# Sparse attention: adding the causal masks on VectorE in the score bank, and a new order of VectorE's work in a head

## The reference

```python
s_c = q @ k_cmp.T * scale            # 31 compressed keys
p_c = masked_softmax(s_c, cmp_end <= t)
s_s = q @ k_sel.T * scale            # selected branch
p_s = masked_softmax(s_s, key <= t)
s_w = q @ k_win.T * scale            # window branch
p_w = masked_softmax(s_w, key <= t)
o = g0 * (p_c @ v_cmp) + g1 * (p_s @ v_sel) + g2 * (p_w @ v_win)
```

## Time and profile before

| | us |
|---|---|
| median of 3 runs | 977.13 (976.85 to 977.81) |
| the profiled execution | 977.82, its span 976.0 |
| PE busy in the span | 943.1 (97%) |
| DVE, ACT, POOL busy | 474.0, 418.0, 442.7 |
| mean granted clock of PE | 0.990 |

### The profile page before, as it was taken

One profiled execution on the slowest core, in us unless ns is written; L12 is line 12 of the kernel. 1 busy time (PEld: TensorE's weight loads), 2 busy tenths in 40 slices (PEclk: granted clock), 3 DMA queues, 4 the chain that ended last, 5 costly groups with the idle time before them and its releaser, 6 DMA issues. The chain is left out here.

```text
span 976.0 us, 15705 instructions
## 1 busy us (share of the span) xinstructions
PE 943.1 (97%) x5718; PEld 821.5 (84%) x5718; DVE 474.0 (49%) x1523; ACT 418.0 (43%) x973; POOL 442.7 (45%) x589
## 2 busy tenths in 40 slices
PE   6999998999999999999999999999899999999798
PEld 6888888999999997888888878888688888888676
DVE  5231028787777774211201126668546666666411
ACT  5353236777777774322422423444233333333310
POOL 2453427887877853333433336668611111111131
PEclk9999999999999999999999999999989999999899
DMA  6332221110111012122652122322100000000031
GB/s 210 110 119 86 79 79 47 47 48 23 36 47 47 13 44 87 44 87 84 142 134 88 44 87 87 93 87 87 43 1 1 2 1 1 2 1 2 1 118 54
DMA packets 39253, 58.84 MB, mean 60 GB/s; under 512 B 8693, under 2 KB 22282, under 8 KB 39178
## 3 DMA queue, kind: packets, MB, share of 16 engines
q1 hardware_dynamic: 39136, 57.84, 18.9%
q10 hardware_dynamic: 42, 0.01, 0.0%
HBM read 55.62 MB, written 2.10 MB: 59 GB/s over the span
## 5 line engine op out<-in xcount | busy, mean ns | idle before, releaser
L1359 POOL TENSOR_TENSOR w_lo<-w_raw,w_hi 128x2048 fp32r<-128x2048 f32 (+1 forms) x26 | 118.4, 4553 | 158.9 <-ACT w_hi L1133 158.9
L95 PE MATMUL bank<-w_hi,h_hi 128*128 128x512 f32 (+2 forms) x480 | 187.2, 390 | 3.0 <-POOL w_lo L1287 1.9
L97 PE MATMUL bank<-w_hi,h_lo 128*128 128x512 f32 (+2 forms) x480 | 183.3, 382 | 0.0
L96 PE MATMUL bank<-w_lo,h_hi 128*128 128x512 f32 (+2 forms) x480 | 183.3, 382 | 0.0
L95 PEld LDWEIGHTS bank<-w_hi,h_hi 128*128 128x128 f32 x480 | 90.3, 188 | 21.3 <-issue 2.6
L97 PEld LDWEIGHTS bank<-w_hi,h_lo 128*128 128x128 f32 x480 | 90.2, 188 | 17.1
L96 PEld LDWEIGHTS bank<-w_lo,h_hi 128*128 128x128 f32 x480 | 90.3, 188 | 15.6
L1925 POOL TENSOR_TENSOR o_c<-o_c,o_sw 128x256 f32<-128x256 f32 x16 | 11.7, 732 | 171.8 <-DVE o_c L1994 171.8
L1133 ACT ACTIVATE w_hi<-w_raw 128x2048 fp32r<-128x2048 f32 (+1 forms) x26 | 49.2, 1891 | 78.9 <-PE bank L97 78.9
L1841 PE MATMUL bank<-kvr,probT 128*128 128x65 f32 x640 | 80.5, 273 | 0.0
L95 PE MATMUL bank<-w_hi,o_hi 128*128 128x512 f32 x192 | 78.2, 407 | 2.1 <-PEq L2023 2.1
(11 more groups left out here) (277 smaller groups left out, 2193.1 us busy)
## 6 DMA issues: line engine op xcount, KB each, us to landing
w_raw<-in_nsa_w_in SPq DMA_DIRECT2D x10, 1024.0 KB, 5.0
w_raw<-in_mla_w_in SPq DMA_DIRECT2D x8, 1024.0 KB, 5.1
w_raw<-in_mla_w_out SPq DMA_DIRECT2D x8, 1024.0 KB, 5.2
w_raw<-in_nsa_w_in SPq DMA_DIRECT2D x8, 984.0 KB, 5.0
w_raw<-in_mla_w_uq SPq DMA_DIRECT2D x8, 576.0 KB, 4.1
w_raw<-in_mla_w_ukv SPq DMA_DIRECT2D x16, 256.0 KB, 2.7
w_raw<-in_nsa_w_out SPq DMA_DIRECT2D x4, 1024.0 KB, 5.0
w_raw<-in_mla_w_in SPq DMA_DIRECT2D x4, 704.0 KB, 5.6
```

The lines of the kernel that those rows point to most:

```text
L95: nc.tensor.matmul(out, a[0], b[0], start=start, stop=False)
L96: nc.tensor.matmul(out, a[0], b[1], start=False, stop=False)
L97: return nc.tensor.matmul(out, a[1], b[0], start=False, stop=stop)
L1359: nc.gpsimd.tensor_tensor(w_lo[g % 2][:, :, 0:width], w_raw[g % 2][:, :, 0:width], w_hi[g % 2][:, :, 0:width].bitcast(F32), ALU.subtract). ...
```

## The change

The six mask matmuls of a head are gone from PE. The last large term of a unit now ends it (stop=True, s_done). A new f32 tile "after" (0 on and below the diagonal, NEG above it, in the turned layout) is made once by GpSimd, and DVE adds it in place in the score bank to the first 128 columns of each branch, one instruction a unit, with a new semaphore s_masked on which ACT's exponential waits. The second branch of units 4 and 5 now starts its accumulation with start=True. On DVE the order of a head becomes: masks 0 and 1, low(n+1), masks 2, 3 and 4, maximum 0 of n+1, mask 5, maximum 1, compressed_max, maxima 2 and 3, compressed_turned, maxima 4 and 5, compressed_sum, leave of tiles 0 to 2, leave of tile 3, compressed_leave.

```diff
--- before.py
+++ after.py
@@ -1699,6 +1699,8 @@
                 c_s = at_slab("c_s", 31, [P, NT, NC])
                 c_e = at_slab("c_e", 31.5, [P, NT, NC])
                 c_eT = at_slab("c_eT", 58, [P, P])
+                after = at_slab("after", 59.25, [P, P])
+                after_set, s_masked = sem("after_set"), sem("s_masked")
                 rowmax = at_slab("rowmax1", 58.5, [P, 2, NT, 2])
                 scored = [at_slab(f"scored{a}", 60 + 2 * a, [P, SEQ]) for a in range(2)]
                 coef = at_slab("coef1", 58.625, [P, NT, 2])
@@ -1762,7 +1764,7 @@
                         j, keys = block_of[u][0], slice(block_of[u][0] * P, (block_of[u][0] + 1) * P)
                         left = left_of(j)
                         dst = score_bank[(U * n + u) % 3][:, w * left:(w + 1) * left]
-                        nc.tensor.matmul(dst, kT_hi[0:DK, b, g, keys], qT_lo[a][:, j * P:], start=w == 0, stop=False)
+                        nc.tensor.matmul(dst, kT_hi[0:DK, b, g, keys], qT_lo[a][:, j * P:], start=True, stop=False)
                         nc.tensor.matmul(dst, kT_lo[:, b, g, keys], qT_hi[a][0:DK, j * P:], start=False, stop=False)
 
                     def large_term(n, u, w, b):
@@ -1771,15 +1773,8 @@
                         j, keys = block_of[u][0], slice(block_of[u][0] * P, (block_of[u][0] + 1) * P)
                         left, rows = left_of(j), DK + 1 + b
                         dst = score_bank[(U * n + u) % 3][:, w * left:(w + 1) * left]
-                        nc.tensor.matmul(dst, kT_hi[0:rows, b, g, keys], qT_hi[a][0:rows, j * P:], start=False, stop=False)
-
-                    def mask(n, u):
-
-                        j, branches = block_of[u]
-                        nb, left = len(branches), left_of(j)
-                        dst = score_bank[(U * n + u) % 3][:, 0:nb * left].rearrange("p (b c) -> p b c", b=nb)[:, :, 0:P]
-                        nc.tensor.matmul(dst, causal, identb[:, :].unsqueeze(1).to_broadcast([P, nb, P]), start=False,
-                                         stop=True).then_inc(s_done, 1)
+                        return nc.tensor.matmul(dst, kT_hi[0:rows, b, g, keys], qT_hi[a][0:rows, j * P:], start=False,
+                                                stop=True)
 
                     def scores(n, u):
                         k = U * n + u
@@ -1787,7 +1782,8 @@
                             pe.wait_ge(exp_done, k - 2)
                         for w, b in enumerate(block_of[u][1]):
                             small_terms(n, u, w, b)
-                            large_term(n, u, w, b)
+                            last = large_term(n, u, w, b)
+                        last.then_inc(s_done, 1)
 
                     def start_scores(n):
 
@@ -1801,9 +1797,7 @@
                         if n == 0:
                             pe.wait_ge(rows_set, 1)
                         for u in range(2):
-                            large_term(n, u, 0, u)
-                        for u in range(2):
-                            mask(n, u)
+                            large_term(n, u, 0, u).then_inc(s_done, 1)
 
                     def compressed_scores(n):
                         a = n % 2
@@ -1855,16 +1849,12 @@
                             turn_q(n + 1)
                         scores(n, 2)
                         scores(n, 3)
-                        mask(n, 2)
-                        mask(n, 3)
                         values(n, 0)
                         scores(n, 4)
-                        mask(n, 4)
                         if more:
                             first_scores(n + 1, 0)
                             first_scores(n + 1, 1)
                         scores(n, 5)
-                        mask(n, 5)
                         compressed_scores(n)
                         values(n, 1)
                         if more:
@@ -1891,7 +1881,7 @@
                         j, branches = block_of[u]
                         wide = len(branches) * left_of(j)
                         at = at_of[j, branches[0]]
-                        act.wait_ge(s_done, k + 1)
+                        act.wait_ge(s_masked, k + 1)
                         nc.scalar.activation(probT[n % 2][:, at:at + wide], score_bank[k % 3][:, 0:wide],
                                              ACT.Exp).then_inc(exp_done, 1)
 
@@ -1919,6 +1909,10 @@
                     o = Order(pool, pool_s)
                     o.link(nc.gpsimd.memset(kT_hi[DK:DK + 2, :, :, :].bitcast(F32), 1.0))
                     nc.gpsimd.memset(kT_hi[DK:DK + 1, 1, :, :].bitcast(F32), 0.0).then_inc(rows_set, 1)
+                    pool.wait_ge(rows_set, 1)
+                    o.link(nc.gpsimd.memset(after[:, :], 0.0))
+                    nc.gpsimd.affine_select(out=after[:, :], in_=after[:, :], compare_op=ALU.is_ge, fill=NEG, base=0,
+                                            pattern=[[1, P]], channel_multiplier=-1).then_inc(after_set, 1)
                     for n in range(H):
                         pool.wait_ge(o_left, 2 * n + 2)
                         pool.wait_ge(cv_left, n + 1)
@@ -1995,25 +1989,41 @@
                                                 c_coef[:, :].unsqueeze(2).to_broadcast([P, NT, DV]),
                                                 ALU.mult).then_inc(cv_left, 1)
 
+                    def mask(n, u):
+                        j, branches = block_of[u]
+                        nb, left = len(branches), left_of(j)
+                        dve.wait_ge(s_done, U * n + u + 1)
+                        at = score_bank[(U * n + u) % 3][:, 0:nb * left].rearrange("p (b c) -> p b c", b=nb)[:, :, 0:P]
+                        nc.vector.tensor_tensor(at, at, after[:, :].unsqueeze(1).to_broadcast([P, nb, P]),
+                                                ALU.add).then_inc(s_masked, 1)
+
                     low(0)
                     for u in range(U):
                         maximum(0, u)
+                    dve.wait_ge(after_set, 1)
                     for n in range(H):
                         more = n + 1 < H
+                        for u in range(2):
+                            mask(n, u)
                         if more:
                             low(n + 1)
+                        for u in range(2, 5):
+                            mask(n, u)
+                        if more:
                             maximum(n + 1, 0)
+                        mask(n, 5)
+                        if more:
                             maximum(n + 1, 1)
                         compressed_max(n)
                         if more:
                             maximum(n + 1, 2)
                             maximum(n + 1, 3)
-                        compressed_sum(n)
-                        leave(n, slice(0, 3), o_most, 2 * n + 1)
                         compressed_turned(n)
                         if more:
                             maximum(n + 1, 4)
                             maximum(n + 1, 5)
+                        compressed_sum(n)
+                        leave(n, slice(0, 3), o_most, 2 * n + 1)
                         leave(n, slice(3, 4), o_last.unsqueeze(1), 2 * n + 2)
                         compressed_leave(n)
```

## The result

The changed kernel takes 1033.47 us (median of 4 runs, 1027.6 to 1037.62), the kernel before beside it 976.99: a ratio of 1.0576 (95% interval 1.0548 to 1.0604). Slower by 5.8%, where 0.8% faster was forecast. The profiled execution took 1037.62, its span is 1035.7.

The account below looks back on a forecast made before the run. PE was taken to bound the heads' stage: 11.37 us of work plus stalls of 0.42 and 0.44 gave 12.23 a head. Taking 0.48 gained over 15 transitions plus the last head, 7.5 us, gave 969.6 from 977.13; range 964 to 978.5.

Parts of the forecast that it names:

- The walk: Timing of one head's hand-overs between PE, ACT and DVE: 12.23 us a head after the change, from 12.75 in the trace.
- a granted clock that falls in the new gaps: Listed sign that the forecast is wrong: PE's clock dropping in the two new waits, ahead of units 3 and 5.
- T: Zero point of a head: start of ACT's activation that puts the maxima into the query's rows.
- Masks off PE: Removing six identity mask matmuls a head with their loads from PE's path saves 0.57 us a head.
- The gap: PE's wait for DVE's last maximum, ahead of turning the maxima (line 1755), goes with DVE's new order: 0.81 us a head.
- Masks on DVE: Six additions a head in PSUM, 0.29 us at 128x128 and 0.42 at 128x256, raising DVE's load by 2.0 us.
- rival 1: DVE's mask chain costs more than it frees: slower, about 982.5 us at double durations; chance 0.12 beyond 979.1.
- Exponential 0: ACT's first exponential of a head, behind DVE's mask 0: forecast to run from T+1.73 to T+2.33, before from T+1.47.
- the stall ahead of unit 3: New PE wait for the bank of exponential 0, forecast at 0.42 us a head.
- The stall ahead of unit 5: New PE wait for exponential 2, late because low(n+1) stands ahead of mask 2 on DVE; forecast at 0.44 us a head.
- the work: PE's work alone in a head, without new stalls: 12.75 - 0.57 - 0.81 = 11.37 us.
- Rival 3: PE is not held by the exponentials: both stalls vanish, 11.37 us a head, 957 us (half: about 963); chance 0.08.

Follow-up runs that it names:

- e9: Changed kernel plus eight throwaway zero matmuls a head on TensorE, queued in the gap ahead of unit 5; 973.1 us, ratio 0.9958.
- e7: Changed kernel with zero mask matmuls back on TensorE for units 4 and 5 only; 970.83 us, ratio 0.9931.
- e1: Kernel before, masks still on TensorE, with only compressed_sum and the leave of tiles 0 to 2 moved behind maxima 4 and 5; 969.86 us, ratio 0.9926.
- e4: Changed kernel with mask 2 moved ahead of low(n+1) on VectorE; 965.7 us, ratio 0.9885.
- e8: e4 with the previous head's leave of tile 3 and compressed_leave moved behind masks 0 and 1; 962.42 us, ratio 0.9864.
- e2: Changed kernel with VectorE's old order (compressed_sum and leave ahead of compressed_turned and maxima 4 and 5); 1034.57 us, ratio 1.0603.
- e6: Changed kernel with zero mask matmuls back on TensorE for units 0 and 1 only; 1021.83 us, ratio 1.0451.
- e5: Changed kernel with all six zero mask matmuls a head back on TensorE and low(n+1)'s subtraction done twice; 1024.34 us, ratio 1.0477.

## Why the prediction was wrong

**What failed.** The walk gave a period, and the sum turned it into a time at the granted clock of before. I had named "a granted clock that falls in the new gaps" among the things that would prove me wrong, yet gave it neither a chance nor a price. The reasoning that let it pass was that the earlier trace rows read 1.00 although each head had a gap of 0.74 us, so two of 0.4 seemed harmless. But the old gap lay behind the compressed values and ahead of the turning of the maxima and the 512-column matmuls of the next head, and the new one lies just ahead of the smallest matmuls of the head (128, 64, 32 and 65 columns), from which, moreover, the masks' 256-column matmuls of units 4 and 5 had been taken. I read this as: where the gap lies counts, and not its length alone. That is argued and not shown, since no run moved a gap of one length with TensorE's other work unchanged.

**Its price** could have been bounded from the trace of the kernel before, whose stage starts at a granted clock of 0.50 (708 to 714). Matmuls of 512 columns start 0.43 us apart there, and 0.23 at 1.00:

```profile
709.92 0.63 PE L1766 MATMUL bank<-qT_hi,kT_lo 96*128 96x512 f32 x1
710.35 0.63 PE L1765 MATMUL bank<-qT_lo,kT_hi 96*128 96x512 f32 x1
...
789.08 0.39 PE L1766 MATMUL bank<-qT_hi,kT_lo 96*128 96x512 f32 x1
789.31 0.65 PE L1774 MATMUL bank<-qT_hi,kT_hi 97*128 97x512 f32 x2
```

So a head lies between 12.2 us and nearly twice that. Measured: 17.02 us a head here, 12.33 in e9 (760.12 to 772.45 of its T rows), so 4.7 us a head; 14 heads make 65.7 us, and the profiled executions of the two are 1037.6 and 972.6, 65.0 apart. The clock is the whole difference between these two. At full clock the forecast of 969.6 stands beside e9's 973.1 and e7's 970.8.

**Masks off PE, 0.57 us a head.** From e1's 12.28 to e4's 11.87, and e4 still has 0.14 us of waiting ahead of unit 3 in it (the load there comes at 786.19, 0.32 behind the one before at 785.87, where 0.18 is the step; in the starts of the matmuls it costs 0.10). So 0.51 to 0.55: right, or 0.06 too much at most.

**The gap, 0.81 us.** Mis-sized: e1 measures 0.47. Of the 0.34 too much, 0.10 is a slip in the sum: 800.82 less 800.00 less one load step of 0.11 is 0.71. Most of the rest is that I gave the two records of line 1826 a load step of 0.11 each. They are plain f32 with 256 columns. TensorE's matmuls at that place in the kernel before, then in e1, where nothing is waited for, and e1's loads:

```profile
799.72 0.65 PE L1826 MATMUL bank<-v_diag,c_eT 128*128 128x256 f32 x2
800.71 0.60 PE L1755 MATMUL bank<-ident,rowmax 128*2 128x128 f32 x4 [0.34 <-DVE rowmax L1947]
```

```profile
796.97 0.65 PE L1826 MATMUL bank<-v_diag,c_eT 128*128 128x256 f32 x2
797.46 0.60 PE L1755 MATMUL bank<-ident,rowmax 128*2 128x128 f32 x4
```

```profile
796.91 0.30 PEld L1826 LDWEIGHTS bank<-v_diag,c_eT 128*128 128x128 f32 x2
797.24 0.52 PEld L1755 LDWEIGHTS bank<-ident,rowmax 128*2 128x2 f32 x4
```

The columns of line 1755 start 0.49 us behind those of line 1826 in e1, where the sum's own steps put them 0.33 apart, and the four loads of line 1755 need 0.52 for the 0.30 in the earlier trace rows: they queue behind columns that still run. So 0.16 us of what I took for idle was TensorE streaming columns of line 1826. The matmul record itself had the nearer number, an idle of 0.34 us where the record of loads has 0.74. The Trainium skill, page FP8 and Floating Point Precision, section TensorE Precision Notes, says that true FP32 makes four passes through the array. The trace agrees: the matmuls of 512 columns above start 0.23 us apart, so four passes of 256 are an estimated 0.46, for the 0.49 measured. The rule would have corrected that part of the term.

**Masks on DVE.** 292 and 433 ns for 0.29 and 0.42: right, so rival 1 did not arise. The result is on its side of zero, but its mechanism isn't the cause. The higher overhead on PSUM that the prediction cites from the Trainium skill, page Perfetto Trace Analysis, section Optimizing Scalar/DVE Operations, does not show here for an f32 addition that reads and writes PSUM.

**The walk.** Exponential 0 came at T+1.51, not 1.73: T itself is 0.3 us later behind the last maximum (line 1826 again), so VectorE's leftovers were out sooner, and the stall ahead of unit 3 was 0.14 at the load and 0.10 in the matmuls, not 0.42. The stall ahead of unit 5 is 0.43 in the record of loads, but part of that lies under columns still running. Its cost is read from unit 5's third matmul, in the changed kernel at full clock and in e4, which has no such stall (T is 722.59 and 784.01):

```profile
727.45 0.27 PE L1776 MATMUL bank<-qT_hi,kT_hi 97*128 97x128 f32 x1
```

```profile
788.52 0.27 PE L1776 MATMUL bank<-qT_hi,kT_hi 97*128 97x128 f32 x1
```

T+4.86 for T+4.51: 0.35, for the 0.44 forecast. So at full clock the changed kernel's head would be 11.87 + 0.35 = 12.22 us, an estimate; e9's 12.33 with its overrun of 0.11 gives the same. The forecast was 12.23. That is luck in part: the work was 0.40 too short (11.37 for 12.28 - 0.51 = 11.77), the two stalls 0.32 and 0.09 too long, and the three errors cancel. Rival 3 (no stalls) was wrong in the change and right as a recipe: e4 and e8 are what it gives, 11.84 to 11.87 with the work at its true length.

**What stays open.** How stall, missing matmuls and the place of a stall trade against each other. Heads from one T to the next, without the first: in the changed kernel, 0.43 us without the masks' matmuls lost the clock in 14 of 14. In e2 the same stall left one head at 1.00 and then lost it in 13. In e6, 0.42 with matmuls added elsewhere (and 0.32 ahead of unit 3) lost it in 10 of 14. In e5, 0.83 with the masks' matmuls in place (and 0.32 ahead of unit 3) lost it in 6 of 14. In e7, 0.30 with those of units 4 and 5 in place, and in e4, no stall without them, none did. These runs order the cases; they give no rule, and why a head with the same stall sometimes keeps its clock they don't show.

## What to carry to other kernels

When a change takes small work off TensorE and makes it wait, cost it at both clock levels: look at what the engine does just ahead of and behind the new wait, and take a stretch of small matmuls behind it as a risk with its own chance (these runs suggest that it counts; they don't prove it). If the clock is lost, first move the wait (here one VectorE instruction: 965.7 for 1033.5 us), and if it can't be moved, filling it with throwaway matmuls is cheap (973.1). And derive a gap's length from when the engine could have gone on, with the passes of its last matmuls counted, not from the idle that the record shows between starts.

## What the runs showed of the hardware

In the changed kernel's heads from 722.59 on, the clock went to 0.50 for 10.2 us of 17.0 although TensorE's loads had not stood still longer than 0.43 us at a time at full clock; for the same kernel with the gap filled it stayed at 1.00. The Trainium skill, page TensorE: Matmul & The Clock Gate, section "A second HAM failure mode: psum-queue depth-cycling", tells of a bf16 kernel with 512 columns in which small idles between groups of matmuls that cycle through PSUM banks make the clock swing between its two levels. The trace agrees: unit 5 waits for a bank, the idle is 0.43 us, and the clock swings once a head. e9 adds that work in that idle was enough to hold it, and e4 that taking the idle away was.
